# A hybrid attention and expert block on one core: two gate exponentials, six dot products and the last steps of one tile take other places in the order of work

## The reference, cut to what matters

```python
v1, i1 = lax.top_k(s1, 16)              # per token and head, two halves of 128 keys
v2, i2 = lax.top_k(s2, 16)
cand = v1[..., :, None] + v2[..., None, :]
sc, pos = lax.top_k(cand.reshape(...), 16)
eidx = take_along_axis(cidx, pos)       # 16 of 128*128 experts, for each of 8 heads
gate = softmax(sc)
act = gelu(einsum('td,thkd->thk', h, u[eidx]))
x = x + einsum('thk,thkd->td', gate * act, v[eidx])
x = x + sigmoid(rmsnorm(x) @ w_pg) * (p @ w_ple)
out = rmsnorm(x)
```

## Time and profile before

| | |
|---|---|
| runs | 1652.03 us median of 3 (1650.39 to 1657.33) |
| the profiled execution | 1648.55 us; its span from first to last instruction 1646.7 us |
| busy | PE 98%, DVE 64%, ACT 26%, POOL 40% of the span |
| TensorE clock granted | 0.996 |
| DMA | 475.62 MB, 289 GB/s over the span |

### The profile page before, as it was taken

The page is one execution under the profiler, slowest core; times in us unless marked ns, Lnnn a source line. Parts: engine busy times, 40 slices in busy tenths (PEclk is TensorE's granted clock), DMA queues, the critical chain, the costliest instruction groups (busy, mean ns, idle before and its releaser), DMA issues.

```text
span 1646.7 us, 18447 instructions
## 1 busy us (share of the span) xinstructions
PE 1608.7 (98%) x6342; PEld 1051.1 (64%) x6342; DVE 1049.9 (64%) x2410; ACT 428.9 (26%) x1262; POOL 665.1 (40%) x707
## 2 busy tenths in 40 slices
PE   8999999999999999999999999999999999999997
PEld 6446444446786788888889999995444444444443
DVE  2012444432279899998879999996655555667645
ACT  2003444350110211111167777770000000000013
POOL 0002445440001473576745555555433344456420
PEclk9999999999999999999999999999999999999999
DMA  5424111105445899999999999999999999999961
GB/s 167 150 82 148 40 39 39 39 26 166 153 144 167 330 358 398 384 409 388 378 409 408 406 406 404 403 391 406 409 409 409 409 410 353 409 409 409 409 242 39
DMA packets 132122, 475.62 MB, mean 289 GB/s; under 512 B 14731, under 2 KB 15755, under 8 KB 132028
## 3 DMA queue, kind: packets, MB, share of 16 engines
q0 software_dynamic: 73728, 268.47, 41.6%
q1 hardware_dynamic: 58300, 205.97, 33.5%
HBM read 471.19 MB, written 3.19 MB: 288 GB/s over the span
## 4 chain that ended last, share of the span: by engine, by line
PE 73%; DVE 13%; POOL 5%; issue 4%; DMA 3%; ACT 1%; DVEq 0%; SPq 0%; POOLq 0%
PE psum L1821 26%; PE psum L1808 10%; PE psum L1632 6%; DVE arena L1291 5%; PE psum L1508 4%; PE psum L1656 3%; PE psum L1708 3%; PE psum L1668 3%; POOL arena L587 3%; PE psum L1795 3%; PE psum L1751 3%; DMA arena<-in_u,eidx 2%; PE psum L1592 2%; PE psum L1607 2%; DVE psum L1312 2%
## 5 line engine op out<-in xcount | busy, mean ns | idle before, releaser
L1808 PE MATMUL psum<-arena 128*128 128x256 f32 x2048 | 454.2, 379 | 8.3 <-issue 3.9
L1821 PE MATMUL psum<-arena 128*128 128x512 f32 x1024 | 440.6, 592 | 2.5 <-DMA arena<-in_vd 1.4
L1808 PEld LDWEIGHTS psum<-arena 128*128 128x128 f32 x2048 | 383.6, 190 | 59.4 <-issue 10.2
L587 POOL DMA_INDIRECT arena<-in_u,eidx x256 | 258.2, 1008 | 375.3 <-DVE arena L1046 169.4
L587 POOL DMA_INDIRECT arena<-in_v,eidx x256 | 259.8, 1015 | 291.0 <-DVE arena L1326 178.5
L1821 PEld LDWEIGHTS psum<-arena 128*128 128x128 f32 x1024 | 194.2, 190 | 247.7 <-issue 241.5
L1291 DVE CUSTOM_DVE_ANT_0 arena<-psum,arena 128x1024 f32<-128x1024 f32 x256 | 301.1, 1220 | 17.7 <-DMA arena<-in_u,eidx 14.3
L1326 DVE SCALAR_TENSOR_TENSOR arena<-arena,wts 128x1024 f32<-128x1024 f32 x172 | 219.3, 1285 | 110.2 <-DMA arena<-in_v,eidx 107.9
L565 POOL TENSOR_SCALAR arena<-arena 128x256 f32<-128x256 f32 (+4 forms) x128 | 105.9, 846 | 251.6 <-DVE arena L1000 192.0
L1632 PE MATMUL psum<-arena 128*128 128x512 f32 x256 | 118.4, 605 | 0.0
L1708 PE MATMUL psum<-arena 128*128 128x256 f32 x512 | 114.0, 382 | 0.1
(11 more groups left out here) (198 smaller groups left out, 1432.2 us busy)
## 6 DMA issues: line engine op xcount, KB each, us to landing
arena<-in_ut SPq DMA_DIRECT2D x128, 512.0 KB
arena<-in_vd SPq DMA_DIRECT2D x128, 512.0 KB
arena<-in_wpack SPq DMA_DIRECT2D x105, 512.0 KB
arena<-in_u,eidx POOLq DMA_INDIRECT x256
arena<-in_v,eidx POOLq DMA_INDIRECT x256
arena<-in_w_pg SPq DMA_DIRECT2D x8, 512.0 KB, 9.1
arena<-in_x SPq DMA_DIRECT2D x4, 512.0 KB, 4.9
arena<-bias_rows SPq DMA_DIRECT2D x8, 256.0 KB, 5.7
```

The costliest lines, as they stand in the source:

```text
L587: G.indirect_dma_start(out=row_slot(n), out_offset=None, in_=a["v"] if values else a["u"], in_offset=bass.IndirectOffsetOnAxis(ap=eidx[:, ...
L1808: last = T.matmul(chunk_scores(c), u[:, k * P:(k + 1) * P], h2T1[:, k, :], start=(k == 0), stop=(k == KC - 1))
L1821: last = T.matmul(ps[VALUE_BANK[t] + h], mixed[:, c, t * P:(t + 1) * P], stream[:, c % SRING, h * HALF:(h + 1) * HALF], start=(c == 0), st ...
```

## The change

Four things move; the computation stays the same.

1. `gate_exp(2)` stands behind the gelu of chunk 28 instead of 40, `gate_exp(3)` behind that of chunk 46 instead of 54.
2. `EARLY_DOTS` is 146 instead of 140. Since the rows per mixing step stay the same, 41 rows of `sum_early` fall into the mixing stage instead of 35, and 6 fewer `accumulate` rows are left for tile 0. `gates(2)` and `gates(3)` stand behind dot 130 instead of 127.
3. The pieces of the top-k stand 6 dots apart up to the eleventh, then 5. Before, they stood behind dots 2, 8, 13, 18, 23, 28, 34, 39, 44, 49, 54, 59, 65, 70, 75, 80, 85, 90, 96, 101, 106, 111, 116; now behind 2, 8, 14, 20, 26, 32, 38, 44, 50, 56, 62, 67, 72, 77, 82, 87, 92, 97, 102, 107, 112, 117, 122.
4. In `accumulate(1, k)`, `add_dense(2)` stands behind row 108 instead of 112, the steps that follow it move with it, and `tail_add(1)` stands behind row 124 instead of 119, `tail_out(1)` behind 126 instead of 122.

```diff
-EARLY_DOTS = 140
+EARLY_DOTS = 146
-TOP_SPAN = 119
+SPARSE_STEPS = 10
-DOT_OF_STEP = [-(-TOP_SPAN * s // TOP_UNITS) + 2 for s in range(TOP_UNITS)]
+DOT_OF_STEP = [2 + 6 * s if s < SPARSE_STEPS else 2 + SPARSE_STEPS + 5 * s for s in range(TOP_UNITS)]
...
-                if c == 40:
+                if c == 28:
                     gate_exp(2)
-                if c == 54:
+                if c == 46:
                     gate_exp(3)
...
-                if k == EARLY_DOTS - 13:
+                if k == EARLY_DOTS - 16:
                     gates(2)
                     gates(3)
...
-                if k == 112:
+                if k == 108:
                     add_dense(2)
...
-                if k == 119:
+                if k == 124:
                     tail_add(1)
-                if k == 122:
+                if k == 126:
                     tail_out(1)
```

More of the change, by code:

```diff
@@ L1383, in _ @@
                 dot(*divmod(k, COLS))
-                step, off = divmod((k - 2) * TOP_UNITS, TOP_SPAN)
-                if off >= TOP_UNITS:
-                    step = -1
+                step = DOT_OF_STEP.index(k) if k in DOT_OF_STEP else -1
                 if 0 <= step < 5:
@@ L1439, in _ @@
                     tail_out(0)
-                if k == 112:
+                if k == 108:
                     add_dense(2)
-                if k == 113:
+                if k == 109:
                     add_dense(3)
                     tail_scale(1)
-                if k == 115:
+                if k == 111:
                     tail_turned(1)
                     tail_scale(2)
-                if k == 116:
+                if k == 112:
                     tail_turned(2)
-                if k == 119:
+                if k == 124:
                     tail_add(1)
-                if k == 122:
+                if k == 126:
                     tail_out(1)
```

## The result

The changed kernel takes 1656.6 us (median of 20 runs, 1651.07 to 1667.77), the one before on the same chip 1651.65 us (20 runs, 1648.37 to 1658.03). The ratio is 1.0034, with a 95% interval of 1.0018 to 1.005. So the change is a small loss of some 5.6 us by the ratio (the medians lie 4.95 us apart). It lies inside the 0.5% that I called no change, and inside my range. But the interval leaves out 1, so these runs do tell the loss from none.

What follows compares the result with a forecast made beforehand. PE's waits were taken as the clock behind 541 us, with DVE and DMA late at the one-hots. +4.3 + 0.4 - 1.0 - 0.85 = +2.85 us on the earlier median 1652.03 gave 1654.9, say 1655 us; range 1649 to 1661.

Steps and rivals of the forecast that it cites:

- PE's list as the clock: From 541 us to the end, whatever holds PE up costs its full length, unless PE would have waited later anyway.
- The limit of 12.7 us: Sum of the six kinds of PE wait behind 541 us that the change can touch; reordering can win no more.
- The six dots and the spacing, +4.3: At PE's first mix: one-hots at 844.5 instead of 840.2 us, +4.3 us; own case 2.5 to 6 late, chance 0.52.
- Rival (a): Before the one-hots: spaced pieces fill the DMA's unused time, DVE's idle 11.2 us vanish; 1648.5 to 1652.5 us, chance 0.2.
- Rival (b): Before the one-hots: DMA's room stays unused, each added dot costs 1.97 us; +10.3 us in all, 1662 us, chance 0.12.
- The exponentials: Near chunk 31: ACT waits 7.0 us for tile 2's arguments, PE newly waits 4.0 us, covered by the one-hots' wait.
- Rival (c): At chunk 62: tile 2's arguments come late, PE arrives after the one-hots; 1657 us if 5 us late, chance 0.08.
- Rival (d): At the exponentials: a table switch also pays a drain, PE's wait is 2.7 us longer; 1657.5 us, chance 0.02.
- The end of the mixing stage, +0.4: Six `sum_early` rows replace six dots on DVE, lengthening PE's wait of 1.1 us by 0.4 us; bounds 0 and 0.9.
- The last block of `v`, -1.0: DVE waits longer at row 108, the DMA is less crowded, PE's 1.4 us wait shrinks by 1.0; bounds 0 and -1.4.
- The tail, -0.85: Tile 1's close comes 5.6 us earlier on DVE; PE wins at most its 1.24 us wait, taken as -0.85 us.
- that second sign: Anywhere in the kernel: the forecast is wrong if PE waits at a place it did not name.

Runs made afterwards that it cites:

- tail_only: The kernel before with only the new places of the last steps of tile 1 (point 4); 1645.55 us, ratio 0.9999 to the kernel before.
- new_146: The changed kernel itself, run once more on another chip beside other variants; 1650.87 us, ratio 1.0032 to the kernel before.
- new_140: The changed kernel with 140 early dots instead of 146; 1637.38 us, ratio 0.9958 to the kernel before.
- new_142: The changed kernel with 142 early dots instead of 146; 1642.81 us, ratio 0.9984 to the kernel before.
- new_152: The changed kernel with 152 early dots instead of 146; 1658.60 us, ratio 1.0071 to the kernel before.
- old_146: The kernel before with only 146 early dots, gates of tiles 2 and 3 behind dot 130; 1655.02 us, ratio 1.0056 to the kernel before.
- space_140: The kernel before with only the new spacing of the top-k pieces, still 140 early dots; 1638.60 us, ratio 0.9957 to the kernel before.
- exps_only: The kernel before with only the two exponentials moved, to chunks 28 and 46; 1646.31 us, ratio 0.9999 to the kernel before.
- warm_146: The changed kernel with 20 unread PE products between chunk 62 and the wait for the one-hots; 1649.94 us, ratio 1.0028 to the kernel before.
- new_144: The changed kernel with 144 early dots instead of 146; 1648.46 us, ratio 1.0021 to the kernel before.

## Why the prediction was right, point by point

- **The number.** 1655.0 was forecast and 1656.6 measured. It is closer than its working was, and that was luck. Against the profiled execution my sum was +2.85 us and the trace shows +7.8. The ratio lies between, at +5.6. The median of before was put 3.5 us above its profile, and the median after is level with its own. That made up the difference.
- **PE's list as the clock.** Right. All the terms below are shifts of PE: +6.94 at the first mix, +8.89 at the first product with `v`, +8.53 behind the last block of `v`, +7.82 at the last gate (1633.19 - 1625.37). The limit of 12.7 us left out the 1.6 us for L740, and counted waits that come and go from run to run (below).
- **The six dots and the spacing, +4.3.** It was +6.9 in the pair of the result and +5.0 between tail_only and new_146. The forecast's own case was one-hots 2.5 to 6 us late: the second lies in it, the pair of the result doesn't. The last piece ended about where I put it, at 805.57 for 806.7. The step that failed is the next one: "two blocks fewer have to pass: 40.4 - 2 x 1.28 = 37.8 us", for "the same 23 rows". The stretch from the last piece to the one-hots took 41.5 us (805.57 to 847.10). The DMA view over that stretch, first before (799.80 to 840.20), then after; q0 carries the gathered rows, q1 the blocks; the second number is MB:

```profile
q0 software_dynamic: 2885, 10.53, 67.1%
q1 hardware_dynamic: 1503, 5.49, 34.1%
```

```profile
q0 software_dynamic: 3092, 11.26, 68.6%
q1 hardware_dynamic: 1504, 5.44, 32.9%
```

PE worked 31.3 us in place of 35.8 there, 1.3 chunks less, and SP issued 9 blocks in place of 11. But the blocks that landed came to the same bytes, 5.44 MB for 5.49, so the 2.6 us that I took off for two blocks were not there. And the rows came to 0.73 MB more, 1.4 rows or 1.8 us at 409 GB/s. Why the ring took the bytes all the same is not shown. The room of the DMA was used about as I took it: I forecast 4.0 us, and from 548 to 606 us the changed kernel moved 355 GB/s in place of 320, which is 35 x 58 / 409 = 5.0 us. From 606 to 700 it gained nothing (394 for 393), where new_140 gained 3.4.
- **The clock, +1.95.** Missing from the sum. I priced a wait of PE at its own length. Over all profiles in which the clock fell ahead of the first mix it is 1.5 to 3.0 us.
- **Rival (a)** (the spacing removes DVE's idle time) did not occur, but it is what happens with 140 dots. **Rival (b)** (each dot at the late pace of 1.97 us) had nearly the right price for a dot, which came to 2.1 to 2.2 us, and left out what the spacing gives back. With 152 dots the loss it spoke of is there.
- **The exponentials.** A wait of 4.0 us was forecast, covered by that for the one-hots. In the changed kernel's own profiles it didn't appear; in new_142 it was 3.58 and in new_152 3.55 us. In exchange I hoped to lose 2.8 us for the gelu and 2.7 of "issue". They are gone in the changed kernel, which has 1.6 and 1.4 us for gelus elsewhere, but the exponentials had not made them: tail_only, old_146 and space_140 have the exponentials at the old places and show neither wait. In the profile of before, the wait of 2.84 us at 765.15 stands behind an idle ACT:

```profile
764.62 0.66 ACT L824 ACTIVATE arena<-psum 128x256 f32<-128x256 f32 x2 [5.88 <-remote]
```

The slack on ACT was right in size, but the table load stands ahead of the wait, which I had put behind it. **Rival (c)** (PE comes later than the one-hots) was not met here, and nearly so in new_142, where PE came at 836.2 and the one-hots at 836.1. **Rival (d)**, with the drain that the Trainium skill states ("ScalarE: Activation LUTs", section "What ACT_TABLE_LOAD costs"), fell: the exponential of exps_only starts at 715.12, 1.29 us after its load at 713.83.
- **The end of the mixing stage, +0.4.** The wait for L1349 is 1.14 us before and after: 0.
- **The last block of `v`, -1.0.** DVE's wait doubled as forecast (16.68 us), but PE's shift fell only from 8.89 to 8.53: -0.4. The wait is 1.05 us instead of 1.4.
- **The tail, -0.85.** -0.71: the shift goes from 8.53 to 7.82. The wait of 1.24 us is gone and one of 0.59 stands for it.
- **What would make it wrong.** The first mix started at 847.84, just inside the 848 that I had set, and PE waited at a place that I hadn't named (5.9 us for L740). By that second sign the forecast's account was wrong, though the time was right. PE had chunk 62 done at the time of before only because two things cancelled. It reached L740 3.4 us earlier and lost 2.9 us less in waits behind it; against that stand 4.4 us more of waiting at L740 and 1.9 us at half clock.

Taking the trace's terms instead of mine: 2.85 + 2.64 (one-hots) + 1.95 (clock) - 0.4 (mixing) + 0.64 (block of `v`) + 0.14 (tail) = 7.82 us, the shift at the last gate and all of the 7.8 us between the two profiled executions.

What stays open is why the spacing is worth 9.0 us at the one-hots with 140 dots and only 2.3 with 146. One part can be read. From the last piece to the one-hots it takes 42.6 us in tail_only and 28.1 in space_140, 14.5 less for the six dots that the spacing puts ahead of the piece. With 146 dots it takes 49.7 us in old_146 and 40.9 in new_146, only 8.8 less. (The piece itself comes 5.5 and 6.5 us later with the new spacing.) The reason is that the last dots of old_146 go at 1.28 us, since PE stands from 829.7 on, so six fewer save less. That is read from single profiles, and the stock of rows behind the last piece was nine dots in new_140 and new_142, seven in warm_146 and five in new_146, and the last two have the same order up to there. Single profiles so differ by some us at this place. The medians put the difference at 7.1 against 3.9 us (1.0056 - 1.0032 of 1645), which their intervals don't separate.

## What to carry to other kernels

The price of one more step depends on what it shares at that moment. Here a dot cost nothing, about 2.2 or about 1.3 us, according to whether the one-hots were early, PE was still taking blocks, or PE stood. So ask first which side arrives first, and try the two sides of that point apart: this change joined a gain of 7 us (the spacing) and a loss of some 13 (the six dots with it), and taken together it read as nearly no difference. And where TensorE waits for some us, add what the clock costs behind the wait, here 1.5 to 3.0 us for waits of 3 to 14 us.

## What the runs showed of the hardware that was not expected

- In the part of the kernel that the change touches, the granted clock fell to 0.50 in or behind waits of PE of 2.20 (space_140, at 1112 us), 3.08 (warm_146), 3.58 (new_142), 4.7 (new_152, for the gates), 5.9 (the changed kernel, L740), 6.3 (exps_only), 7.9, 8.8, 9.6, 10.1, 14.0 and 14.2 us. It didn't in those of 2.26 and 2.84 us (before) and 3.55 us (new_152). One wait is the same in all thirteen profiles, 2.27 us for DVE's L1059 near 542 us with one of 0.48 behind it. The clock fell behind it in seven of them and not in the other six. So the length of a short wait doesn't settle it.
- The cost at the first mix, counted as the stretch from there to the first product with `v` against the 282.9 us of new_140, was 1.5 to 3.0 us and did not grow with the wait: 2.8 us behind 6.3 (exps_only), 1.5 behind 8.8 (new_144), 3.0 behind 14.0 (new_146), 1.6 behind 14.2 (old_146).
- Executions of one kernel differ in step with their clock: new_142 took 1638.2 and 1639.1 us where the mean clock was 0.999, and 1640.7 to 1647.2 where it was 0.995 to 0.997.
- The table load of an exponential runs before the wait for its arguments (712.07 to 713.35, the wait behind it), so half of the switch is hidden by it.
- In the profile of the changed kernel seven instructions of ACT start behind idle times that the trace lays to something remote. The 4.43 us ahead of L740 are one of them; two more are gelus at 711.56 and 716.00 us, behind 4.73 and 4.06 us where 3.07 is usual. The profile of before has seven such releases as well. The eleven later profiles have none, and in nine of these PE is through with chunk 62 by 831.5 us instead of 838. The cause stays open.
